# Output projection, middle norms and first two MLP slabs by thirds of the tokens

## What is computed

```python
def trunk_layer(x, ...):
    a, k_new, v_new, ki_new, conv_new = token_mixers(rms_norm(x, gains[0]), ...)   # ends with m @ w_o
    x = x + rms_norm(a, gains[1])
    f = jnp.square(jax.nn.relu(rms_norm(x, gains[2]) @ w_up)) @ w_down
    x = x + rms_norm(f, gains[3])

def rms_norm(x, g):
    xf = x.astype(jnp.float32)
    y = xf * lax.rsqrt(jnp.mean(xf * xf, axis=-1, keepdims=True) + EPS)
    return (y * g.astype(jnp.float32)).astype(x.dtype)
```

## Time and profile before

| | |
|---|---|
| runs | 3700.28, 3700.87, 3704.8 us; median 3700.87 |
| profiled execution | 3699.1 us, span 3697.3 us |
| TensorE busy (matmul) | 3375.3 us, 91% of the span |
| VectorE busy | 1903.4 us, 51% |
| GpSimd busy | 1185.1 us, 32% |
| ScalarE busy | 721.0 us, 20% |
| mean granted clock | 0.948 |

### The profile page before, as it was taken

How to read it: one execution, slowest core, us unless ns; L and a number is a source line. 1 busy time by engine, 2 the same in 40 slices (tenths; PEclk the granted TensorE clock), 3 DMA queues, 4 the chain that set the end, 5 groups by cost and what they waited for, 6 DMA issues and landing times.

```text
span 3697.3 us, 48934 instructions
## 1 busy us (share of the span) xinstructions
PE 3375.3 (91%) x19604; PEld 3201.4 (87%) x19604; DVE 1903.4 (51%) x3006; ACT 721.0 (20%) x1113; POOL 1185.1 (32%) x497
## 2 busy tenths in 40 slices
PE   3989997999979999999749899979998799999996
PEld 2989996669969999999739899956798799999996
DVE  4249997644174242424372599976442733323244
ACT  2330112541121010101123201125402200101010
POOL 6013331004334443434350133310044344334441
PEclk9989997999979999999869899979999799999998
DMA  4111222012211111112121112220132111111121
GB/s 165 47 57 42 71 91 98 23 42 99 93 65 46 42 44 45 45 45 91 38 90 53 54 44 76 93 87 24 42 105 100 59 43 43 45 45 45 40 93 59
DMA packets 75359, 233.95 MB, mean 63 GB/s; under 512 B 12816, under 2 KB 25456, under 8 KB 73712
## 3 DMA queue, kind: packets, MB, share of 16 engines
q1 hardware_dynamic: 33552, 122.57, 11.0%
q10 hardware_dynamic: 41696, 109.88, 8.0%
HBM read 176.37 MB, written 56.05 MB: 63 GB/s over the span
## 4 chain that ended last, share of the span: by engine, by line
PE 70%; DVE 23%; issue 3%; ACT 2%; ACTq 1%; POOL 1%; DMA 0%; SPq 0%; DVEq 0%; POOLq 0%
PE PS L410 52%; DVE PASS L1268 11%; PE PS L476 5%; PE PS L623 4%; PE PS L594 3%; PE PS L611 2%; PE PS L506 2%; DVE X L1078 1%; DVE TC L1288 1%; DVE HN L1078 1%; PE PS L446 1%; DVE H L1089 1%; DVE TC L1283 1%; PE PS L490 1%; DVE RANK L1322 1%
## 5 line engine op out<-in xcount | busy, mean ns | idle before, releaser
L410 PE MATMUL PS<-H,W 128*128 128x358 f32 x9792 | 1644.9, 330 | 62.9 <-DVE H L1096 53.6
L410 PEld LDWEIGHTS PS<-H,W 128*128 128x128 f32 x9792 | 1635.0, 191 | 69.7 <-ACT H L1011 39.8
L346 POOL TENSOR_TENSOR W<-RAW,ones 128x1024 fp32r<-128x1024 f32 x216 | 419.3, 1941 | 2314.8 <-PE PS L410 1940.6
L410 PE MATMUL PS<-A,W 128*128 128x358 f32 x5760 | 950.0, 327 | 0.0
L410 PEld LDWEIGHTS PS<-A,W 128*128 128x128 f32 x5760 | 948.4, 189 | 1.5 <-issue 1.5
L348 POOL TENSOR_TENSOR W<-RAW,W 128x1024 fp32r<-128x1024 f32 x216 | 613.1, 2838 | 16.9
L1268 DVE TENSOR_SCALAR_CACHE_REDUCE PASS<-SC,TC,CST 48x176 bf16<-48x176 f32 x496 | 408.7, 882 | 2.2
L1457 DVE TENSOR_TENSOR X<-X,PS 128x1074 f32 (+1 forms) x64 | 81.5, 1274 | 593.7 <-PE PS L410 593.7
L476 PE MATMUL PS<-WQ,H 128*128 128x364 f32 (+1 forms) x1296 | 238.4, 340 | 49.0 <-DVE H L1089 19.1
L476 PEld LDWEIGHTS PS<-WQ,H 128*128 128x128 f32 (+1 forms) x1296 | 211.8, 184 | 64.7 <-issue 35.6
L1445 DVE TENSOR_TENSOR SQ<-SQ,RS 128x1074 f32<-128x1074 f32 x64 | 118.1, 1845 | 259.3 <-ACT SQ L1024 258.8
(11 more groups left out here) (133 smaller groups left out, 2274.7 us busy)
## 6 DMA issues: line engine op xcount, KB each, us to landing
RAW<-in_w_slab SPq DMA_DIRECT2D x216, 512.0 KB, 3.6
x_keep<-X ACTq DMA_DIRECT2D x32, 537.0 KB, 2.8
gates<-GS ACTq DMA_DIRECT2D x32, 537.0 KB, 2.9
XT<-x_keep ACTq DMA_DIRECT2D x8, 2148.0 KB, 12.6
RAW<-in_w_qkv SPq DMA_DIRECT2D x16, 546.0 KB, 3.7
GA<-gates ACTq DMA_DIRECT2D x16, 537.0 KB, 3.6
GB<-gates ACTq DMA_DIRECT2D x16, 537.0 KB, 4.5
qs_keep<-QH ACTq DMA_DIRECT2D x16, 512.0 KB, 2.6
```

What stands on the lines that cost most here:

```text
L346: g_.tensor_tensor(hi, raw, one, ALU.mult).then_inc(hi_split, 1)
L410: mm = nc.tensor.matmul(PS[:, b0 + c, 0:CW], W[:, s, w, k, :], act[:, a, k, c * CW:(c + 1) * CW], start=(first and w == 0 and a == 0), sto ...
```

## The change

The output projection is done in 24 items (`ITEMS`), each one output tile j for one third c, 24 matmuls into one PSUM bank (`item`): first tile 0 of all three thirds with k outside, then tiles 1 to 7 of third 0, of third 1, of third 2. Six banks are used in turn. As each tile's weights are read three times at different times, the split weights of tiles 1 to 7 are held in `WR`, seven matrices of 8 KB a partition on the region `r_a`. The two MLP slabs behind it are done by thirds too (`up_item`).

ScalarE squares and copies each item (`wo_item`), VectorE adds it (`add_item`). Each norm is done for one third at a time: six events a layer (`EVENTS`), each with three matmuls for the sums (`chunk_sums`), mean and root (`std_c`), reciprocal and one instruction for three diagonals (`inv_rms_c`), three matmuls for the broadcast (`chunk_broadcast`) and a copy (`rs_c`). The residual rows of a third (`mid_rows` on VectorE, `h2_rows` on ScalarE) stand two by two between the items of the next third; those of the last third stand behind the items. VectorE adds all squares of the second norm (`add_mid`), GpSimd none. The residual is loaded and stored by thirds, three DMAs of 1.47 MB each way in place of two loads of 2.2 MB and eight stores of 0.54 MB. The accumulator `X` is no longer cleared: the first block's down slabs copy to it. The cores of the diff:

```diff
+PIECE = P - 8
+PARTS = (0, PIECE - 1, CW - PIECE)
+ITEMS = [(0, c) for c in range(NCH)] + [(j, c) for c in range(NCH) for j in range(1, KT)]
+LAST = [NCH + (KT - 1) * (c + 1) - 1 for c in range(NCH)]
+EVENTS = [(0, 0), (0, 1), (1, 0), (0, 2), (1, 1), (1, 2)]
...
-                split_slabs(1, S_MLP // 2 + 1)
-
-                add_squares(l * 4 + 2)
-                split_slabs(S_MLP // 2 + 1, NSLAB // 2)
+                split_slabs(1, S_WO // 2)
+
+                for j in range(KT + 2):
+                    i = S_WO + j
+                    g_.wait_ge(raw_in[i % 2], (l * (NRAW // 2) + KT // 2 + i // 2 + 1) * 16)
+                    if j == 0:
+                        g_.wait_ge(slab_done, l * NDONE + S_WO - 1)
+                        hi, lo = W[:, 0, 0, :, :], W[:, 0, 1, :, :]
+                    elif j < KT:
+                        g_.wait_ge(slab_done, l * NDONE + S_WO)
+                        hi, lo = WR[:, j - 1, 0, :, :], WR[:, j - 1, 1, :, :]
+                    else:
+                        g_.wait_ge(item_done, l * len(ITEMS) + NCH)
+                        g_.wait_ge(slab_done, l * NDONE + S_WO)
+                        hi, lo = W[:, j - KT, 0, :, :], W[:, j - KT, 1, :, :]
...
+            def item(w, bank_, j, c, act, ks, first, last):
+
+                for k in ks:
+                    for h, a in ((0, 0), (0, 1), (1, 0)):
+                        mm = nc.tensor.matmul(PS[:, bank_, 0:CW], w[:, h, k, :], act[:, a, k, c * CW:(c + 1) * CW],
+                                              start=(k == first and h == 0 and a == 0), stop=(k == last and h == 1))
+                return mm
...
+                for k in range(KT):
                     pe.wait_ge(m_hi, l * NMERGE + k + 1)
                     pe.wait_ge(m_lo, l * NMERGE + k + 1)
...
+                    for c in range(NCH):
+                        last = item(W[:, 0], c, 0, c, H, [k], 0, KT - 1)
+                        if k == KT - 1:
+                            last.then_inc(item_done, 1)
+                for n, (j, c) in enumerate(ITEMS):
+                    if j == 0:
+                        continue
+                    slab_in(l, S_WO + j)
+                    if n >= 6:
+                        pe.wait_ge(item_drained, l * len(ITEMS) + n - 5)
+                    last = item(WR[:, j - 1], n % 6, j, c, H, range(KT), 0, KT - 1)
+                    last.then_inc(item_done, 1)
+                    if n == LAST[0] + 1:
+                        chunk_sums(l, 0)
+                    if n == LAST[0] + 3:
+                        chunk_broadcast(l, 0)
+                    if n == LAST[1] + 1:
+                        chunk_sums(l, 1)
+                    if n == LAST[1] + 3:
+                        chunk_broadcast(l, 1)
+                        chunk_sums(l, 2)
+                    if n == LAST[1] + 5:
+                        chunk_broadcast(l, 2)
...
+                slab_in(l, S_MLP)
+                up_item(0, 0, range(KT))
+                chunk_sums(l, 3)
+                slab_in(l, S_MLP + 1)
+                up_item(1, 0, range(KT))
+                chunk_broadcast(l, 3)
+                chunk_sums(l, 4)
+                up_item(0, 1, range(KT))
+                chunk_broadcast(l, 4)
+                up_item(1, 1, range(KT))
+                up_item(0, 2, range(KT)).then_inc(slab_done, 1)
+                up_item(1, 2, range(KT)).then_inc(slab_done, 1)
+                chunk_sums(l, 5)
...
+                for n in range(len(ITEMS)):
+                    wo_item(n)
+                    if n in LAST:
+                        mid_load(LAST.index(n))
+                    if n == LAST[0] + 1:
+                        std_c(0)
+                    if n == LAST[0] + 3:
+                        rs_c(0)
+                    if LAST[0] + 4 <= n <= LAST[1]:
+                        h2_rows(0, range(2 * (n - LAST[0] - 4), 2 * (n - LAST[0] - 4) + 2))
...
+                std_c(3)
+                rs_c(3)
+                std_c(4)
+                h2_rows(2, range(2))
+                rs_c(4)
+                h2_rows(2, range(2, KT))
...
+                for j in js:
+                    V_.scalar_tensor_tensor(X[:, j, cols], X[:, j, cols],
+                                            cst["gain"][:, l * 32 + 8 + j:l * 32 + 9 + j],
+                                            RS[:, cols], ALU.mult, ALU.mult).then_inc(mid_scaled, 1)
+                    if j:
+                        lo(j - 1)
+                        add_mid(l, c, j - 1)
+                    dve.wait_ge(mid_scaled, i + j + 1)
+                    V_.tensor_tensor(X[:, j, cols], X[:, j, cols], XT2[:, j, cols], ALU.add).then_inc(x_mid, 1)
...
+                for n in range(len(ITEMS)):
+                    add_item(l, n)
+                    if n == LAST[0] + 1:
+                        inv_rms_c(l, 0)
+                    if LAST[0] + 4 <= n <= LAST[1]:
+                        mid_rows(l, 0, range(2 * (n - LAST[0] - 4), 2 * (n - LAST[0] - 4) + 2))
+                    if n == LAST[1] + 1:
+                        inv_rms_c(l, 1)
+                    if n == LAST[1] + 3:
+                        inv_rms_c(l, 2)
+                    if LAST[1] + 4 <= n <= LAST[2]:
+                        mid_rows(l, 1, range(2 * (n - LAST[1] - 4), 2 * (n - LAST[1] - 4) + 2))
+                inv_rms_c(l, 3)
+                mid_rows(l, 2, range(2))
+                inv_rms_c(l, 4)
+                mid_rows(l, 2, range(2, KT))
+                inv_rms_c(l, 5)
```

More of the change, by code:

```diff
@@ L666, in _ @@
[L666 to L688, removed]
@@ L718, in rest_of_block @@
                             slab(l, g, s, 3 * s, A)
-                with pe.Fori(0, NFB - 1) as b:
+                for s in range(2):
+                    slab_in(l, S_MLP + 2 + s)
+                    pe.wait_ge(up_drained, l * NFB * 8 + 2 + s + 1)
+                    slab(l, 1, s, 3 * s, H)
+                    if s == 0:
+                        chunk_broadcast(l, 5)
+                rest_of_block(0, 2)
+                up_pair(1)
+                with pe.Fori(1, NFB - 1) as b:
                     rest_of_block(b)
@@ L1007, in _, with wo_item @@
[L1007 to L1019 removed]
+                def wo_item(n):
+                    j, c = ITEMS[n]
+                    act.wait_ge(item_done, l * len(ITEMS) + n + 1)
+                    if l or n >= 3:
+                        act.wait_ge(sqc_added, l * len(ITEMS) + n - 2)
+                    nc.scalar.activation(SQC[:, n % 3, :], PS[:, n % 6, 0:CW], ACT.Square).then_inc(sqc_made, 1)
+                    copy(X[:, j, c * CW:(c + 1) * CW], PS[:, n % 6, 0:CW]).then_inc(item_drained, 1)
@@ L1020, in _, with up_evacuations @@
+                for s in range(2):
+                    act.wait_ge(slab_done, l * NDONE + D_MLP + s + 1)
+                    act.wait_ge(a_lo, l * 32 + s + 1)
+                    relu(s, s)
+                    if s == 0:
+                        std_c(5)
+                rs_c(5)
+                for s in range(2):
+                    a_hi_row(s, slice(s, s + 1), s)
+                def up_evacuations(b, g0):
+                    with act.Fori(g0, 4) as g:
                         for s in range(2):
@@ L1452, in up, with down @@
                                              ALU.subtract).then_inc(a_lo, 1)
-                def down(b, j, s):
+                def down(b, j, s, first=False):
                     row_ = X[:, bass.ds(j, 1), :].rearrange("p a (c n) -> p (a c) n", c=NCH)
-                    dve.wait_ge(slab_done, l * NSLAB + S_MLP + b * 16 + 8 + j + 1)
-                    V_.tensor_tensor(row_, row_, bank(3 * s), ALU.add).then_inc(down_drained, 1)
-                with dve.Fori(0, NFB - 1) as b:
+                    dve.wait_ge(slab_done, l * NDONE + D_MLP + b * 16 + 8 + j + 1)
+                    if first:
+                        V_.tensor_copy(row_, bank(3 * s)).then_inc(down_drained, 1)
+                    else:
+                        V_.tensor_tensor(row_, row_, bank(3 * s), ALU.add).then_inc(down_drained, 1)
+                up(0)
+                with dve.Fori(0, 4) as g:
+                    for s in range(2):
+                        down(0, g * 2 + s, s, True)
+                with dve.Fori(1, NFB - 1) as b:
                     up(b)
```

316 lines of the change are left out of this document (210 added, 106 removed).

## The result

| | before | after |
|---|---|---|
| median us | 3702.73 (3700.28 to 3704.8, 4 runs) | 3640.01 (3637.84 to 3643.0, 4 runs) |
| span of the profiled execution, us | 3697.3 | 3636.9 |
| mean granted clock | 0.948 | 0.954 |
| VectorE, ScalarE, GpSimd busy, us | 1903.4, 721.0, 1185.1 | 1926.7, 740.8, 1137.6 |

The ratio is 0.9831, with a 95% interval from 0.9814 to 0.9848: 62.7 us less. The forecast was 3641, from 3612 to 3674.

What follows compares the result with a forecast made beforehand. TensorE bounds the kernel, so time leaves only where it stands still. Savings of 31.2 us in layer 0 and 28.4 in layer 1, together 59.6, take 3699.1 to 3639.5; with 1.8 for the median, 3641 us, range 3612 to 3674.

Steps and rivals of the forecast that it cites:

- Where the idle time was: Stretch behind the output projection: 58.1 + 55.2 = 113 us of the two layers are TensorE waiting.
- Same-bank accumulation at no cost: Projection items: consecutive matmuls in one PSUM bank stay at 165 ns, 24 items 95.1 us, cost 0.
- the third rival: Projection items: accumulating 24 in a row into one bank makes matmuls slower, up to 3879 us; chance 0.05.
- Held weights at no cost: GpSimd's splits of tiles 1 to 7: 5.1 us each, seventh ready at 941, wanted at 942.1; cost 0.
- Prices of a third: Instructions of 358 columns, interpolated: VectorE 0.53 and 0.59 us, ScalarE 0.48 and 0.58 us.
- The tie of the queues: Residual rows between items: VectorE and ScalarE wait for each other, 6.4 us an item against 3.96.
- the signs: List of what a trace would show, such as a longest wait of 6 to 8 us in up item (0, third 2).
- The clock: Last up item before slab 3: half of the price between full and half clock, 2 us.
- What goes at nothing: Removed work: memset of X (7.2 us of VectorE), GpSimd's adds and the loops' waits are off the path, 0.

Runs made afterwards that it cites:

- e1: Changed kernel with no residual row between the items, the rows of all thirds standing behind them; 3716.67 us, ratio to before 1.0034.
- e2: Changed kernel with VectorE's next-row scaling and last row's low part and square moved ahead of the add of the item's square; 3624.10 us, ratio 0.9784.
- e3: Changed kernel with extra unused matmuls of 358 columns on TensorE where it waits; 3628.30 us, ratio to before 0.9799.
- e8: Changed kernel with one more GpSimd multiplication (1.9 us) ahead of each of the seven held tiles' splits; 3661.81 us, ratio to before 0.9884.
- e7: Kernel before without the memset of X, the first block's down slabs copied instead of added; 3704.65 us, ratio 1.0.
- e4: Kernel before with VectorE instead of GpSimd adding the squares of the second norm; 3688.27 us, ratio to before 0.9961.
- e5: Kernel of e2 with the last third's squares of the second norm summed by TensorE instead of added on VectorE; 3611.53 us, ratio to before 0.9749.
- e6: Changed kernel with the last third's squares added by GpSimd in place of VectorE; 3641.73 us, ratio to before 0.9829.

## Why the prediction was right

The forecast was 59.6 us of saving, and 62.7 us came between the medians. The path, the waits and their order came as written; the agreement to 1 us is in part luck, as the end of this section shows. By its steps:

**Where the idle time was** and that it could be hidden: right. e1 shows it from the other side.

**Same-bank accumulation at no cost**: right. 164 ns a matmul in items against 165 in slabs; the third rival is out. Its count was a little off: tile 0 has its k steps outside the thirds, so its matmuls change bank every three, and 2 x 648 matmuls, not 2 x 720, accumulate 24 in a row into one bank.

**Held weights at no cost**: right. The seventh tile was ready sooner than put, at 4.5 us a split in place of 5.1. I think that GpSimd had less of VectorE's company, but no run takes this apart. Its last split in the changed kernel:

```profile
934.97 1.90 POOL L373 TENSOR_TENSOR WR<-RAW,ones 128x1024 fp32r<-128x1024 f32 x1
936.94 2.55 POOL L375 TENSOR_TENSOR WR<-RAW,WR 128x1024 fp32r<-128x1024 f32 x1
```

Ready at 939.5 and wanted at 919.43 + 6 x 3.96 = 943.2: 3.7 us of slack for the 1 us forecast.

**Prices of a third**: right to 0.03 us, against the interpolation from the earlier trace rows. The changed kernel's groups by shape, 960 to 1045 (busy us, mean ns of one, idle time ahead):

```profile
L1323 DVE SCALAR_TENSOR_TENSOR H<-X,CST,H 128x358 fp32r<-128x358 f32 x24 | 14.2, 590 | 4.2 <-ACT H L1135 4.2
L1328 DVE SCALAR_TENSOR_TENSOR X<-X,CST,RS 128x358 f32<-128x358 f32 x24 | 14.0, 585 | 1.5 <-ACT RS L1126 1.5
L1335 DVE TENSOR_TENSOR X<-X,XT 128x358 f32<-128x358 f32 x24 | 12.6, 526 | 0.1
```

A third costs 0.53 us, three of them 1.58 us for the 1.28 us of one whole; thirds aren't free, but the price was small beside what they hide.

**The tie of the queues**: right in kind, 5.96 us a pair for 6.4 forecast. e2 shows that the order of the two queues makes it. What I had missed is that consecutive VectorE instructions overlap by some 0.09 us (of 0.53 us each, they start 0.44 us apart), so every chain is a little shorter than its sum. It comes back in the rows of the last third (2.13 us for 2.25) and in TensorE's waits: 2.31 for 3.3 us ahead of the second sum, 1.58 for 2.6 us ahead of the last third's, and 4.9 us in all within up item (0, third 2), where the signs had 6 to 8 us. Slab 3 was forecast 144.9 us behind the projection's start and came at 142.3.

**The clock**: the term that was mis-sized. I took 2 us, for the last item alone. It fell behind three waits and cost time behind two of them, and e3 gives it as 3.8 us a layer. In the middle one the slow item (5.71 us) only takes up a wait: TensorE waits 0.62 us for the diagonal where I had forecast 3 us. A wait of 2.31 us was enough (9.63 us for items 18 and 19), which the earlier trace rows left open; e8 shows that it need not be. Its miss of 1.8 us a layer and the long chains of the step before went against each other: with 3.8 us of clock in the sum, the forecast of slab 3 would have been 4.4 us too late, and not 2.6.

**Behind slab 3**: a wait that the prediction hadn't listed, 1.27 us ahead of the fifth MLP slab (TensorE for ScalarE's relu). It is no loss against before, which waited 2.18 us at its own place.

**What goes at nothing**: the memset, right (e7). GpSimd's adds of the second norm I had put off the path as well, and there I was wrong in the working, not in the sum: e4 shows 14 to 15 us for taking them out of the old row loop. The forecast counted the new stretch from its own prices, so that gain was in it under another name: rows of 2.25 us a third instead of a third of 5.8 us plus the cost of cutting.

**The luck in it**: in the stretch that the prediction sums, 59.6 us were forecast and 64.8 us came, 5.2 us more (33.9 for 31.2 in layer 0, 30.9 for 28.4 in layer 1). 4.4 us were lost again outside it, which is in no term and which another execution need not show, and the median of the kernel before came out at 3702.73 us, 1.9 us above the one that the forecast started from. So the median agrees to 1 us because misses of both signs went against each other, inside the stretch and outside; the working is good to about 3 us a layer, not to 1.

## What to carry to other kernels

Cut a norm barrier along the tokens when the product ahead of it can be done in pieces: what the pieces hide is the work of all but the last, and the last one's rows are what is left to shorten (e5). When two in-order engines hand rows to each other, walk the two queues instruction by instruction: an item's square behind the wrong row cost 1.4 us each time, and moving three instructions ahead of its add gave 16 us (e2). Before giving work to an idle engine, look at what it does to the instructions beside it; here that was dearer than doing the work on the busy one in e4, and no cheaper in e6. Where a wait can't be taken away, unused matmuls in it can keep the clock: 3.8 us a layer here (e3).

## What the runs showed of the hardware

A TensorE wait of 2.31 us in otherwise dense work was followed by a stretch at a granted clock of 0.61, part of it at 1.2 GHz, and by 1.7 us of loss; twelve matmuls in its place, whose results nobody uses, kept the clock at 1.00 (e3). Behind a wait of 1.58 us, 24 matmuls took 5.71 us where full clock makes 3.96. I had taken such waits as free of it, but for the last item. The length of a wait alone does not decide, though: waits of 2.20 and 2.23 us in e8 left the clock at 1.00, and in e3 24 matmuls behind one of 2.14 us took 4.16 us. What does decide, no run here takes apart.

The Trainium skill (TensorE: Matmul & The Clock Gate, Part 1, HAM oscillation) says that a wait between bursts of matmuls that is long enough sends the clock to half, and that this is paid again at each such wait. The trace agrees that waits bring it on and that it can come back several times in a layer; that it comes at every wait of some length from 1.58 to 2.41 us, it does not bear out.

An instruction of 358 columns on VectorE beside one of 0.83 us on GpSimd took 1.15 us in place of 0.53 (e6), 0.62 us more, three quarters of GpSimd's instruction. At full size it was 2.19 us more (3.47 for 1.28) beside one of 2.57 us, so the contention does not go away with short instructions.
